# Value products of an even and an odd head alternate between the two column halves, with four buffers for turned probabilities

## The chip, the cores and the metric

The kernel runs on one core of one Trainium2 chip. The metric is the time of one execution on the device in microseconds (us); lower is better. A core has a matrix engine (TensorE, "PE" in the profile; its weight loads are listed apart as "PEld"), VectorE ("DVE"), ScalarE ("ACT"), GpSimd ("POOL") and SyncE ("SP", which only issues DMAs here). Each engine runs its own instructions in their order and waits for others on semaphores.

## The reference

One layer of a decoder on 256 tokens of width 1024. What matters here is the attention in the middle of it:

```python
h = rms_norm(x, g);  columns = h @ w_in          # queries, keys, values, gates of all branches
o_c = softmax(q k_cmp / 8 + bias) @ v_cmp        # 8 heads, 15 compressed blocks (o_c, o_s, o_w: "NSA")
o_s = softmax(q k_sel / 8 + bias, causal) @ v_sel  # 8 heads; at 256 tokens all blocks are selected
o_w = softmax(q k_win / 8 + bias, causal) @ v_win  # 8 heads
o_nsa = g0 * o_c + g1 * o_s + g2 * o_w           # gates by head and token
o_m = softmax(q k / 8 + bias, causal) @ v        # 4 heads ("moba")
o_x = softmax(q mk / 8) @ mv                     # 4 heads, 256 memory tokens ("mem")
merged = sum_i sigmoid(gate_i) * (o_i @ w_i);  x = x + rms_norm(merged @ w_mix_out)
x = x + rms_norm((silu(h @ w_gate) * (h @ w_up)) @ w_down)
```

All of it is in 32-bit floats.

## The kernel before

The wide products (`w_in`, the gates, the output projections, the feed-forward part) are each done as three products in the type fp32r: every operand is split into a high and a low part, ScalarE making the high part of a weight (`hi`, L485), VectorE the low part (`lo`, L767), and TensorE adds high by high, low by high and high by low (L1143 to L1145). The unit of this work is `sub`: 12 matmuls of 512 columns.

The attention lies in the middle of the program. Its 24 softmax products are 24 jobs, one for each head and branch (`job_plan`): 4 moba, 4 mem, then for each of the 8 NSA heads a "sel" job and a "win" job. They are run by the same loop `for n in range(JOBS + 2)` on each engine, 26 steps long, and TensorE does in step n, in this order:

- `scores(n)`: the logits of job n, four fp32r matmuls into `sbank` (L1277, L1278);
- one `sub` of a gate product, 12 matmuls into `acc`, which fills the time in which the others work on the softmax;
- `turn(n - 1)`: three or four transposes of the finished probabilities of job n - 1 from `sx` into the PSUM bank `ptb` (L1328);
- `values(n - 2)`: the products of values and turned probabilities of job n - 2.

Meanwhile VectorE adds the bias and takes the maximum (L997, L1005, L1007), ScalarE takes the exponential (L655), VectorE makes the factor (L1016, L1017, L1020), GpSimd scales the probabilities (L440), and after the transposes ScalarE copies `ptb` to SBUF as `pts`, in two buffers (`evac_pt`, L635). In step 4 four more transposes turn the compressed probabilities of all heads (L1366), after a wait for the copy of job 2.

A value product is in full fp32. The values of a head, 128 tokens by 64 dimensions, are the stationary operand; the turned probabilities, 128 tokens by 256 queries, move through. Its result takes 64 of the 128 partitions of `ob`: the lower half for an even head, the upper for an odd one. So it uses 64 of the array's 128 columns ("128*64" in the profile). A moba or win job has a product of 256 columns (L1354) and one of 128 (L1356), a mem job two of 256, a sel job three: one of 256 for the compressed branch (L1343), 256 and 128. The win job of a head adds to what its sel job left. When both halves of `ob` are complete (`ends_pair`), ScalarE and VectorE split the bank into `oh` and `ol` (L640, L1037), and the next pair's first product waits for that.

The lines that the text speaks of:

Of the kernel before, what the change touches and what calls it, by code (L numbers as in the profile page):

```python
# [25 lines left out]
F32 = mybir.dt.float32  # L26
F32R = mybir.dt.float32r
ALU = mybir.AluOpType
ACT = mybir.ActivationFunctionType
AX = mybir.AxisListType.X  # L30

P = 128
SEQ = 256
TILES = SEQ // P
D = 1024
KD = D // P
HD = 64
SCALE = HD ** -0.5
NSA_H, GROUPS, HPG = 8, 2, 4
# [13 lines left out]
C_QM, C_KM, C_VM, C_QX, C_GATES = 1304, 1560, 1816, 2072, 2328  # L53
ATT_W = C_GATES

SLICE = 512
# [11 lines left out]
JOBS = 24  # L68
# [3 lines left out]
Q_NSA, Q_MOBA, Q_MEM, Q_HEADS = 0, 8, 12, 16  # L72
# [11 lines left out]
def job_plan():  # L84

    jobs = []
    for m in range(MOBA_H):
        jobs.append(("moba", m, Q_MOBA + m, K_MOBA + m, NSA_H + m))
    for m in range(MEM_H):
        jobs.append(("mem", m, Q_MEM + m, K_MEM + m, None))  # L90
    for h in range(NSA_H):
        for kind, first in (("sel", K_SEL), ("win", K_WIN)):
            jobs.append((kind, h, Q_NSA + h, first + h // HPG, h))
    return jobs


def pair_of(job):

    return job // 2 if job < 8 else 4 + (job - 8) // 4


def ends_pair(job):

    return job % 2 == 1 if job < 8 else (job - 8) % 4 == 3
# [5 lines left out]
def t_count(job):  # L110

    return job + 1 if job < CMP_SLOT - 1 else job + 2
# [7 lines left out]
def build_layer(nc, a, out, g_scratch):  # L120
    jobs = job_plan()
# [12 lines left out]
    with ExitStack() as ctx:  # L134
        def sb(name, shape, dt=F32, stack=ctx):
            return stack.enter_context(nc.sbuf_tensor(name, shape, dt))
# [37 lines left out]
        with ExitStack() as s:  # L174

            pat = sb("pat", [P, TILES, 4 * SLICE], F32, s)
            pct = sb("pct", [P, GROUPS, SEQ], F32, s)
            kvm = sb("kvm", [P, TILES, 2 * 256], F32, s)
            with ExitStack() as early:
                x0 = sb("x0", [P, TILES, D], F32, early)  # L180
            qst = sb("qst", [P, Q_HEADS, SEQ], F32R, s)
            khh = sb("khh", [P, K_HEADS, SEQ], F32R, s)
            klo = sb("klo", [P, K_HEADS, SEQ], F32R, s)
            tb = sb("tb", [P, BIAS_H, 256], F32, s)
            tbc = sb("tbc", [P, TILES, NSA_H, 16], F32, s)
            with ExitStack() as early:
                rel = sb("rel", [BUCKETS, BIAS_H], F32, early)
                onehot = sb("onehot", [BUCKETS, SEQ], F32, early)
                grow = sb("grow", [BIAS_H, G_W], F32, early)
            with ExitStack() as early:  # L190
                kvc = sb("kvc", [P, 2, SEQ], F32, early)
                hx = sb("hx", [P, 3, 4 * NCMP], F32, early)
                hidk = sb("hidk", [P, GROUPS * NCMP], F32, early)
                hidv = sb("hidv", [P, GROUPS, HPG, 32], F32, early)
                gcmp = sb("gcmp", [P, 2, PAIRS, GROUPS * NCMP], F32, early)
            sx = sb("sx", [P, 2, 512], F32, s)
            pts = sb("pts", [P, 2, 512], F32, s)
            post = sb("post", [P, 2, CMP_LEN], F32, s)
            c_km = C_KM - SLICE
            pcz = pat[:, :, c_km:c_km + GROUPS * HPG * 32].rearrange("p t (g i c) -> p t g i c", g=GROUPS, i=HPG)  # L200
            w2k = sb("w2k", [CMP_HID, 2, HD], F32, s)
            w2v = sb("w2v", [CMP_HID, HD], F32, s)
            ckeys = sb("ckeys", [P, GROUPS, 2, 16], F32R, s)
            vcz = pat[:, :, 0:HPG * HD].rearrange("p g (i d) -> p g i d", i=HPG)
            xc = sb("xc", [P, TILES, NSA_H, 16], F32, s)
            cst = sb("cst", [P, 4, TILES * NSA_H], F32, s)
            gsig = sb("gsig", [P, TILES, 3 * NSA_H], F32, s)
            jst = sb("jst", [P, 5, JOBS, TILES], F32, s)
# [12 lines left out]
        ptb = psum("ptb", [P, 512])  # L221
        ob = psum("ob", [P, 512])
# [28 lines left out]
        qk_pe, qk_hi, qk_ev = sem("qk_pe"), sem("qk_hi"), [sem("qk_ev0"), sem("qk_ev1")]  # L251
# [6 lines left out]
        t_done, te_done, pv_done = sem("t_done"), sem("te_done"), sem("pv_done")  # L258
        oh_done, ol_done = sem("oh_done"), sem("ol_done")
# [35 lines left out]
        def half_rows(side):  # L295
            return slice(HD * side, HD * side + HD)
# [99 lines left out]
        def _(pool):  # L396
# [44 lines left out]
                                                  ALU.mult, ALU.mult)  # L441
                ins.then_inc(p_done, 1)

            pool.wait_ge(pv_done, JOBS)
            nc.gpsimd.dma_start(xs[:], xf).then_inc(xsd, 16)
            nc.gpsimd.dma_start(gpost[:], bass.AP(a["post_mix_g"].tensor, 0, [[0, P], [1, D]])).then_inc(gpostd, 16)
            for n in range(2):
# [23 lines left out]
        def _(act):  # L471
# [157 lines left out]

            def evac_pt(n):  # L630
                act.wait_ge(t_done, t_count(n))
                if n >= 2:
                    act.wait_ge(pv_done, n - 1)
                w = 512 if jobs[n][0] == "mem" else 384
                nc.scalar.activation(pts[:, n % 2, 0:w], ptb[:, 0:w], ACT.Copy).then_inc(te_done, 1)  # L635

            def evac_o(n):
                if ends_pair(n):
                    act.wait_ge(pv_done, n + 1)
                    nc.scalar.activation(oh[:, pair_of(n), :], ob[:, 0:256], ACT.Copy).then_inc(oh_done, 1)  # L640

            for n in range(JOBS + 2):
# [117 lines left out]
        def _(dve):  # L760
# [59 lines left out]
                                               ALU.mult, ALU.subtract).then_inc(meml_done, 1)  # L820

            nc.vector.memset(eps[:], EPS).then_inc(eps_set, 1)

            def reciprocals(i, slot):
                nc.vector.reciprocal(rstd[:, slot, :], small[:, 2 * i:2 * i + 2]).then_inc(rstd_done, 1)
# [313 lines left out]
        def _(pe):  # L1139
# [188 lines left out]
                    ins = nc.tensor.transpose(ptb[:, dst:dst + P], sx[:, n % 2, src:src + P], ident)  # L1328
                ins.then_inc(t_done, 1)

            def values(n):

                kind, h = jobs[n][0:2]
                starts = kind != "win"
                ends = kind != "sel"
                if n == 0:
                    pe.wait_ge(qk_ev[1], 4)
                elif ends_pair(n - 1):
                    pe.wait_ge(ol_done, pair_of(n))
                dst = ob[HD * (h % 2):HD * (h % 2) + HD]  # L1340
                if kind == "sel":
                    g = h // HPG
                    nc.tensor.matmul(dst[:, 0:256], vcz[:, g, h % HPG, :], pct[:, g, :], start=True, stop=False)  # L1343
                    starts = False
                if kind == "moba":
                    c = pat_col(C_VM + HD * h)
                    v = [pat[:, t, c:c + HD] for t in range(2)]
                elif kind == "mem":
                    v = [kvm[:, t, 256 + HD * h:256 + HD * h + HD] for t in range(2)]
                else:  # L1350
                    c = pat_col((C_VS if kind == "sel" else C_VW) + HD * (h // HPG))
                    v = [pat[:, t, c:c + HD] for t in range(2)]
                pe.wait_ge(te_done, t_count(n))
                nc.tensor.matmul(dst[:, 0:256], v[0], pts[:, n % 2, 0:256], start=starts, stop=False)  # L1354
                c0 = 0 if kind == "mem" else P
                nc.tensor.matmul(dst[:, c0:256], v[1], pts[:, n % 2, 256:512 - c0], start=False, stop=ends).then_inc(pv_done, 1)  # L1356

            for n in range(JOBS + 2):
                if n < JOBS:
# [19 lines left out]
                    qk_batch(QK_LAST, 6, [col(C_QX), col(C_QX + P)])  # L1379
                if 1 <= n <= JOBS:  # L1380
                    turn(n - 1)
                if n >= 2:
                    values(n - 2)

            def merged_banks(first, count):
# [110 lines left out]
```

## Time and profile before

| | |
|---|---|
| time, median of 3 runs | 448.36 us (448.05 to 448.48) |
| time of the profiled execution | 449.88 us |
| its span | 448.1 us |
| granted TensorE clock, mean | 0.995 |
| TensorE matmul busy | 430.5 us, 96% |
| VectorE, ScalarE, GpSimd busy | 271.7, 240.2, 57.4 us |
| the attention loop | about 92 to 209 us |

A time in a row of the timeline is the start of the first and the duration from there to the end of the last of the instructions merged in it. Matmuls are pipelined, so their durations overlap: what a matmul costs TensorE is the distance from its start to the next one's. In brackets stands how long the engine was idle before, and what released it. In rows of the trace a fp32 value product appears as two matmuls, each with its weight load (so "x2"); a transpose and a fp32r matmul appear as one.

### The profile page before, as it was taken

How to read it: one execution, taken by the hardware profiler on the slowest of the kernel's cores; microseconds unless marked ns; L12 is line 12 of the kernel's file. 1: busy time of each engine (PE TensorE's matmuls, PEld its weight loads, DVE VectorE, ACT ScalarE, POOL GpSimd, SP SyncE). 2: the span in 40 equal slices, each digit the busy share in tenths (PEclk: the TensorE clock that was granted, in tenths of full speed). 3: DMA queues.
4: the chain of work that ended last, by engine and by line, in shares of the span. 5: the costliest groups of instructions: out<-in, count | busy, mean ns of one | idle time of the engine just before them, and what ended most of it. 6: DMA issues, size and time to landing. Idle time of an engine off the chain costs nothing.

```text
span 448.1 us, 5855 instructions
## 1 busy us (share of the span) xinstructions
PE 430.5 (96%) x2044; PEld 346.3 (77%) x2044; DVE 271.7 (61%) x463; ACT 240.2 (54%) x410; POOL 57.4 (13%) x88
## 2 busy tenths in 40 slices
PE   5999979999999999999999989999999999999995
PEld 3788869977777777777778678888888888888883
DVE  4764984886556648553975956555555555545534
ACT  5655854577566564564364667444445444634321
POOL 5110720011211111111700410000000000000000
PEclk9999989999999999999999999999999999999999
DMA  8999952344522243424755347655555555555202
GB/s 303 392 327 375 364 194 95 100 135 140 189 94 96 94 113 113 151 96 148 273 166 182 123 153 236 221 186 179 175 176 175 177 179 177 181 185 193 81 1 94
DMA packets 51840, 78.80 MB, mean 176 GB/s; under 512 B 2044, under 2 KB 28424, under 8 KB 51816
## 3 DMA queue, kind: packets, MB, share of 16 engines
q1 hardware_dynamic: 50200, 73.79, 49.9%
q0 software_dynamic: 1328, 4.43, 3.0%
q8 instruction: 14, 0.23, 0.2%
q10 hardware_dynamic: 288, 0.28, 0.2%
q14 instruction: 10, 0.08, 0.1%
HBM read 77.42 MB, written 1.07 MB: 175 GB/s over the span
## 4 chain that ended last, share of the span: by engine, by line
PE 87%; DVE 5%; issue 2%; DMA 2%; ACT 1%; POOL 0%; SPq 0%; POOLq 0%; DVEq 0%; ACTq 0%
PE acc L1145 24%; PE acc L1144 24%; PE acc L1143 24%; PE ob L1354 3%; PE sbank L1277 2%; DMA raw<-in_w_in 2%; PE ptb L1328 2%; DVE wl L767 2%; PE ob L1261 2%; PE ob L1356 1%; PE sbank L1278 1%; PE ptb L1434 1%; PE ob L1343 1%; ACT wh L485 1%; PE sbank L1247 1%
## 5 line engine op out<-in xcount | busy, mean ns | idle before, releaser
L767 DVE TENSOR_TENSOR wl<-raw,wh 128x1024 fp32r<-128x1024 f32 (+1 forms) x129 | 158.3, 1234 | 92.3 <-ACT wh L485 92.1
L485 ACT ACTIVATE wh<-raw 128x1024 fp32r<-128x1024 f32 (+1 forms) x129 | 133.9, 1045 | 95.1 <-PE acc L1145 87.8
L1143 PE MATMUL acc<-wh,xh 128*128 128x512 f32 (+1 forms) x380 | 149.0, 392 | 0.6 <-DVE wl L767 0.4
L1145 PE MATMUL acc<-wh,xl 128*128 128x512 f32 (+1 forms) x380 | 149.0, 392 | 0.0
L1144 PE MATMUL acc<-wl,xh 128*128 128x512 f32 (+1 forms) x380 | 148.6, 391 | 0.0
L1143 PEld LDWEIGHTS acc<-wh,xh 128*128 128x128 f32 x380 | 72.4, 191 | 16.4 <-issue 2.2
L1145 PEld LDWEIGHTS acc<-wh,xl 128*128 128x128 f32 x380 | 71.4, 188 | 14.8
L1144 PEld LDWEIGHTS acc<-wl,xh 128*128 128x128 f32 x380 | 71.5, 188 | 13.8
L440 POOL TENSOR_SCALAR sx<-sx,jst 128x256 f32<-128x256 f32 (+1 forms) x48 | 20.2, 433 | 113.6 <-DVE jst L1017 64.1
L1143 PE MATMUL acc<-wh,ah 128*128 128x512 f32 x88 | 34.3, 390 | 0.0
L1145 PE MATMUL acc<-wh,al 128*128 128x512 f32 x88 | 34.3, 389 | 0.0
L1144 PE MATMUL acc<-wl,ah 128*128 128x512 f32 x88 | 34.2, 389 | 0.0
L655 ACT ACTIVATE sx<-sx,jst 128x128 f32<-128x128 f32 (+1 forms) x40 | 17.9, 449 | 21.4 <-DVE jst L1007 21.4
L997 DVE TENSOR_TENSOR sx<-sbank,tb 128x128 f32<-128x128 f32 (+1 forms) x40 | 12.4, 351 | 20.4 <-PE sbank L1278 20.4
L635 ACT ACTIVATE pts<-ptb 128x384 f32<-128x384 f32 (+1 forms) x24 | 12.1, 506 | 17.6 <-PE ptb L1328 17.6
L1144 PEld LDWEIGHTS acc<-wl,ah 128*128 128x128 f32 x88 | 16.5, 188 | 3.4
L1145 PEld LDWEIGHTS acc<-wh,al 128*128 128x128 f32 x88 | 16.5, 188 | 3.4
L1143 PEld LDWEIGHTS acc<-wh,ah 128*128 128x128 f32 x88 | 16.5, 188 | 3.4
L737 ACT ACTIVATE silu<-acc,rstd 128x256 f32<-128x256 f32 x22 | 10.3, 475 | 12.4 <-PE acc L1145 12.4
L1117 DVE SCALAR_TENSOR_TENSOR act_tok<-acc,rstd,silu 128x256 f32<-128x256 f32 x22 | 10.5, 481 | 7.4 <-ACT silu L737 7.4
L1277 PE MATMUL sbank<-khh,qst 128*128 128x256 f32 (+1 forms) x48 | 14.6, 329 | 0.0
L1278 PE MATMUL sbank<-klo,qst 128*128 128x256 f32 (+1 forms) x48 | 13.2, 278 | 0.0
(190 smaller groups left out, 455.8 us busy)
## 6 DMA issues: line engine op xcount, KB each, us to landing
raw<-in_w_in SPq DMA_DIRECT2D x19, 1024.0 KB
raw<-in_w_ffn_gate SPq DMA_DIRECT2D x22, 512.0 KB
raw<-in_w_ffn_up SPq DMA_DIRECT2D x22, 512.0 KB
raw<-in_w_ffn_down SPq DMA_DIRECT2D x22, 512.0 KB
raw<-in_w_mix_out SPq DMA_DIRECT2D x4, 1024.0 KB
raw<-in_w_mem_kv SPq DMA_DIRECT2D x2, 1024.0 KB
raw<-in_w_nsa_o SPq DMA_DIRECT2D x2, 1024.0 KB
tb<-g_scratch SPq DMA_DIRECT2D x1, 1536.0 KB, 17.1
```

Source lines behind the costliest of these rows:

```text
L440: ins = nc.gpsimd.tensor_scalar(sx[:, n % 2, lo:hi], sx[:, n % 2, lo:hi], jst[:, 4, n, t:t + 1], 1.0, ALU.mult, ALU.mult)
L485: nc.scalar.activation(wh[:, k, :, 0:w], raw[:, slot, 2 * half:2 * half + 2, 0:w], ACT.Copy).then_inc(hi_done, 1)
L635: nc.scalar.activation(pts[:, n % 2, 0:w], ptb[:, 0:w], ACT.Copy).then_inc(te_done, 1)
L655: ins = nc.scalar.activation(sx[:, n % 2, lo:hic], src[:, n % 2, lo:hic], ACT.Exp, bias=jst[:, 1, n, t:t + 1], scale=SCALE, accum_out=jst[ ...
L767: nc.vector.tensor_tensor(wl[:, k, :, 0:w], raw[:, slot, 2 * half:2 * half + 2, 0:w], wh[:, k, :, 0:w].bitcast(F32), ALU.subtract).then_in ...
L997: nc.vector.tensor_tensor(sx[:, n % 2, c0:c1], sbank[:, n % 2, c0:c1], tb[:, bh, c1 - c0 - 1::-1], ALU.add).then_inc(dve_c, 1)
L1143: nc.tensor.matmul(bank[:, 0:w], h[:, k, c], wh[:, slot, s, 0:w], start=first, stop=False)
L1144: nc.tensor.matmul(bank[:, 0:w], h[:, k, c], wl[:, slot, s, 0:w], start=False, stop=False)
L1145: return nc.tensor.matmul(bank[:, 0:w], l[:, k, c], wh[:, slot, s, 0:w], start=False, stop=last)
L1277: nc.tensor.matmul(dst, qst[:, q, cols], high, start=True, stop=False)
L1278: return nc.tensor.matmul(dst, qst[:, q, cols], low, start=False, stop=True)
L1354: nc.tensor.matmul(dst[:, 0:256], v[0], pts[:, n % 2, 0:256], start=starts, stop=False)
```

## The change

The jobs of heads h and h + 1 are put side by side: sel h, sel h + 1, win h, win h + 1. The value products are no longer done one job in each step, but for two jobs in every second step (n odd, from step 3 to step 25). The products of the two jobs alternate: first of the even head into the lower half of `ob`, first of the odd head into the upper half, then the second of each, and so on. For this, four buffers hold turned probabilities: the two of `pts`, now 2 x 256 columns each, and two regions of `pat` whose queries have been used by then. `evac_pt` copies all 512 columns of `ptb` always (before: 384 for all but mem jobs), so `ptb` is set to zero once at the start. `pv_done` counts pairs, and `evac_pt` waits on it from job 4 on. The first value product of each pair waits for the turned probabilities of both jobs.

```diff
--- before.py
+++ after.py
@@ -88,9 +88,10 @@
         jobs.append(("moba", m, Q_MOBA + m, K_MOBA + m, NSA_H + m))
     for m in range(MEM_H):
         jobs.append(("mem", m, Q_MEM + m, K_MEM + m, None))
-    for h in range(NSA_H):
+    for h in range(0, NSA_H, 2):
         for kind, first in (("sel", K_SEL), ("win", K_WIN)):
-            jobs.append((kind, h, Q_NSA + h, first + h // HPG, h))
+            for i in (h, h + 1):
+                jobs.append((kind, i, Q_NSA + i, first + i // HPG, i))
     return jobs
 
 
@@ -194,13 +195,15 @@
                 hidv = sb("hidv", [P, GROUPS, HPG, 32], F32, early)
                 gcmp = sb("gcmp", [P, 2, PAIRS, GROUPS * NCMP], F32, early)
             sx = sb("sx", [P, 2, 512], F32, s)
-            pts = sb("pts", [P, 2, 512], F32, s)
+            pts = sb("pts", [P, 2, TILES, 256], F32, s)
             post = sb("post", [P, 2, CMP_LEN], F32, s)
             c_km = C_KM - SLICE
             pcz = pat[:, :, c_km:c_km + GROUPS * HPG * 32].rearrange("p t (g i c) -> p t g i c", g=GROUPS, i=HPG)
             w2k = sb("w2k", [CMP_HID, 2, HD], F32, s)
             w2v = sb("w2v", [CMP_HID, HD], F32, s)
             ckeys = sb("ckeys", [P, GROUPS, 2, 16], F32R, s)
+            c_qm, c_qx = C_QM - SLICE, 3 * SLICE + C_QX - 4 * SLICE
+            turned = [pts[:, 0], pts[:, 1], pat[:, :, c_qm:c_qm + 256], pat[:, :, c_qx:c_qx + 256]]
             vcz = pat[:, :, 0:HPG * HD].rearrange("p g (i d) -> p g i d", i=HPG)
             xc = sb("xc", [P, TILES, NSA_H, 16], F32, s)
             cst = sb("cst", [P, 4, TILES * NSA_H], F32, s)
@@ -441,7 +444,7 @@
                                                   ALU.mult, ALU.mult)
                 ins.then_inc(p_done, 1)
 
-            pool.wait_ge(pv_done, JOBS)
+            pool.wait_ge(pv_done, JOBS // 2)
             nc.gpsimd.dma_start(xs[:], xf).then_inc(xsd, 16)
             nc.gpsimd.dma_start(gpost[:], bass.AP(a["post_mix_g"].tensor, 0, [[0, P], [1, D]])).then_inc(gpostd, 16)
             for n in range(2):
@@ -629,14 +632,13 @@
 
             def evac_pt(n):
                 act.wait_ge(t_done, t_count(n))
-                if n >= 2:
-                    act.wait_ge(pv_done, n - 1)
-                w = 512 if jobs[n][0] == "mem" else 384
-                nc.scalar.activation(pts[:, n % 2, 0:w], ptb[:, 0:w], ACT.Copy).then_inc(te_done, 1)
+                if n >= 4:
+                    act.wait_ge(pv_done, n // 2 - 1)
+                nc.scalar.activation(turned[n % 4], ptb[:].rearrange("p (t q) -> p t q", t=2), ACT.Copy).then_inc(te_done, 1)
 
             def evac_o(n):
                 if ends_pair(n):
-                    act.wait_ge(pv_done, n + 1)
+                    act.wait_ge(pv_done, n // 2 + 1)
                     nc.scalar.activation(oh[:, pair_of(n), :], ob[:, 0:256], ACT.Copy).then_inc(oh_done, 1)
 
             for n in range(JOBS + 2):
@@ -820,6 +822,7 @@
                                                ALU.mult, ALU.subtract).then_inc(meml_done, 1)
 
             nc.vector.memset(eps[:], EPS).then_inc(eps_set, 1)
+            nc.vector.memset(ptb[:], 0.0)
 
             def reciprocals(i, slot):
                 nc.vector.reciprocal(rstd[:, slot, :], small[:, 2 * i:2 * i + 2]).then_inc(rstd_done, 1)
@@ -1328,20 +1331,9 @@
                     ins = nc.tensor.transpose(ptb[:, dst:dst + P], sx[:, n % 2, src:src + P], ident)
                 ins.then_inc(t_done, 1)
 
-            def values(n):
+            def value_operands(n):
 
                 kind, h = jobs[n][0:2]
-                starts = kind != "win"
-                ends = kind != "sel"
-                if n == 0:
-                    pe.wait_ge(qk_ev[1], 4)
-                elif ends_pair(n - 1):
-                    pe.wait_ge(ol_done, pair_of(n))
-                dst = ob[HD * (h % 2):HD * (h % 2) + HD]
-                if kind == "sel":
-                    g = h // HPG
-                    nc.tensor.matmul(dst[:, 0:256], vcz[:, g, h % HPG, :], pct[:, g, :], start=True, stop=False)
-                    starts = False
                 if kind == "moba":
                     c = pat_col(C_VM + HD * h)
                     v = [pat[:, t, c:c + HD] for t in range(2)]
@@ -1350,10 +1342,27 @@
                 else:
                     c = pat_col((C_VS if kind == "sel" else C_VW) + HD * (h // HPG))
                     v = [pat[:, t, c:c + HD] for t in range(2)]
+                c0 = 0 if kind == "mem" else P
+                return [(v[0], turned[n % 4][:, 0], 0), (v[1], turned[n % 4][:, 1, 0:256 - c0], c0)]
+
+            def values(n):
+
+                kind = jobs[n][0]
+                if n == 1:
+                    pe.wait_ge(qk_ev[1], 4)
+                elif ends_pair(n - 2):
+                    pe.wait_ge(ol_done, pair_of(n))
                 pe.wait_ge(te_done, t_count(n))
-                nc.tensor.matmul(dst[:, 0:256], v[0], pts[:, n % 2, 0:256], start=starts, stop=False)
-                c0 = 0 if kind == "mem" else P
-                nc.tensor.matmul(dst[:, c0:256], v[1], pts[:, n % 2, 256:512 - c0], start=False, stop=ends).then_inc(pv_done, 1)
+                work = [value_operands(n - 1), value_operands(n)]
+                if kind == "sel":
+                    for w, (_k, h, *_r) in zip(work, jobs[n - 1:n + 1]):
+                        w.insert(0, (vcz[:, h // HPG, h % HPG, :], pct[:, h // HPG, :], 0))
+                for i in range(len(work[0])):
+                    for side in range(2):
+                        v, p, c0 = work[side][i]
+                        ins = nc.tensor.matmul(ob[half_rows(side), c0:256], v, p, start=(i == 0 and kind != "win"),
+                                               stop=(i == len(work[0]) - 1 and kind != "sel"))
+                ins.then_inc(pv_done, 1)
 
             for n in range(JOBS + 2):
                 if n < JOBS:
@@ -1379,7 +1388,7 @@
                     qk_batch(QK_LAST, 6, [col(C_QX), col(C_QX + P)])
                 if 1 <= n <= JOBS:
                     turn(n - 1)
-                if n >= 2:
+                if n >= 3 and n % 2:
                     values(n - 2)
 
             def merged_banks(first, count):
```

TensorE's instructions around a sel job, before, with the semaphores that they wait for (`te_done`: turned probabilities copied; `p_done`: probabilities scaled; `ol_done`: `ob` free; `e_done`: exponentials taken):

```order
L1328 MATMUL ptb<-const,sx 128x128 [waits te_done,p_done]
L1328 MATMUL ptb<-const,sx 128x128 x2
L1343 MATMUL ob<-pct,pat 64x256 [waits ol_done]
L1354 MATMUL ob<-pts,pat 64x256 [waits te_done]
L1356 MATMUL ob<-pts,pat 64x128
L1277 MATMUL sbank<-khh,qst 128x128 [waits e_done]
```

The same place in the changed kernel, the end of the step in which a pair of sel jobs is multiplied:

```order
L1331 MATMUL ptb<-const,sx 128x128 [waits te_done,p_done]
L1331 MATMUL ptb<-const,sx 128x128 x2
L1363 MATMUL ob<-pct,pat 64x256 [waits te_done,ol_done]
L1363 MATMUL ob<-pct,pat 64x256
L1363 MATMUL ob<-pts,pat 64x256 x2
L1363 MATMUL ob<-pts,pat 64x128 x2
L1280 MATMUL sbank<-khh,qst 128x128 [waits e_done]
```

The step before it now goes from the transposes straight to the next scores. In the row of `x2` the two products belong to the two heads, one in each half. Near the start of the loop, TensorE's end of step 3 and start of step 4 read so in the changed kernel:

```order
L1331 MATMUL ptb<-const,sx 128x128 [waits te_done,p_done]
L1331 MATMUL ptb<-const,sx 128x128 x2
L1363 MATMUL ob<-pts,pat 64x256 [waits te_done,qk_ev1]
L1363 MATMUL ob<-pts,pat 64x256
L1363 MATMUL ob<-pts,pat 64x128 x2
L1280 MATMUL sbank<-khh,qst 128x256 [waits e_done]
L1281 MATMUL sbank<-klo,qst 128x256
L1280 MATMUL sbank<-khh,qst 128x256
L1281 MATMUL sbank<-klo,qst 128x256
L1375 MATMUL ptb<-const,pat 128x128 [waits te_done,cmp_dve]
```

The last row is the transposes of the compressed probabilities (L1366 before); they stand where they stood, but step 2 ahead of them has lost its value products to step 3.

## Rows read from the trace of the kernel before

**Rows 1.** The page: busy time of the engines, the costliest matmul group.
```profile
PE 430.5 (96%) x2044; PEld 346.3 (77%) x2044; DVE 271.7 (61%) x463; ACT 240.2 (54%) x410; POOL 57.4 (13%) x88
...
L1143 PE MATMUL acc<-wh,xh 128*128 128x512 f32 (+1 forms) x380 | 149.0, 392 | 0.6 <-DVE wl L767 0.4
```

**Rows 2.** Busy time of the engines in the attention loop: us, busy (instructions), clock, DMA.
```profile
92.00:208.00 116.00, 116.00 (x581) 87.95 (x580) 71.01 (x190) 69.85 (x166) 20.20 (x48) 1.00 0.37 119
```

**Rows 3.** Timeline of TensorE: transposes and next scores with no value products between.
```profile
95.17 0.49 PE L1328 MATMUL ptb<-const,sx 128*128 128x128 f32 x3
95.41 0.31 PE L1277 MATMUL sbank<-khh,qst 128*128 128x128 f32 x1
```

**Rows 4.** The same with the value products of a win job.
```profile
180.22 0.49 PE L1328 MATMUL ptb<-const,sx 128*128 128x128 f32 x3
180.64 0.65 PE L1354 MATMUL ob<-pts,pat 128*64 128x256 f32 x2
181.12 0.38 PE L1356 MATMUL ob<-pts,pat 128*64 128x128 f32 x2
181.43 0.33 PE L1277 MATMUL sbank<-khh,qst 128*128 128x128 f32 x1
```

**Rows 5.** The same with those of a sel job.
```profile
184.80 0.49 PE L1328 MATMUL ptb<-const,sx 128*128 128x128 f32 x3
...
185.70 0.59 PE L1354 MATMUL ob<-pts,pat 128*64 128x256 f32 x2
186.13 0.38 PE L1356 MATMUL ob<-pts,pat 128*64 128x128 f32 x2
186.44 0.33 PE L1277 MATMUL sbank<-khh,qst 128*128 128x128 f32 x1
```

**Rows 6.** The same with those of a mem job, which has four transposes.
```profile
127.45 0.60 PE L1328 MATMUL ptb<-const,sx 128*128 128x128 f32 x4
...
128.98 0.33 PE L1277 MATMUL sbank<-khh,qst 128*128 128x128 f32 x1
```

**Rows 7.** Instructions on `ob`: count, duration ns min/median/max, first and last start.
```profile
L1354 PE MATMUL ob<-pts,pat x40: 379/379/431, 99.2 to 208.3; 128*64 128x256 f32 x40
...
L1343 PE MATMUL ob<-pct,pat x16: 379/404/431, 137.5 to 204.1; 128*64 128x256 f32 x16
...
L1354 PE MATMUL ob<-pts,kvm x8: 379/404/430, 118.2 to 133.0; 128*64 128x256 f32 x8
```

**Rows 8.** Timeline of the weight loads within the win job's value products.
```profile
180.64 0.19 PEld L1354 LDWEIGHTS ob<-pts,pat 128*64 128x64 f32 x2 [0.17 <-issue]
180.91 0.35 PEld L1356 LDWEIGHTS ob<-pts,pat 128*64 128x64 f32 x2
```

**Rows 9.** Timeline around steps 2 to 4, all engines.
```profile
98.77 0.55 PE L1328 MATMUL ptb<-const,sx 128*128 128x128 f32 x3
...
100.48 0.82 POOL L440 TENSOR_SCALAR sx<-sx,jst 128x128 f32<-128x128 f32 x2 [1.77 <-DVE jst L1020]
...
103.39 0.49 PE L1328 MATMUL ptb<-const,sx 128*128 128x128 f32 x3
...
104.15 0.47 ACT L635 ACTIVATE pts<-ptb 128x384 f32<-128x384 f32 x1
...
105.17 0.60 PE L1366 MATMUL ptb<-const,pat 128*128 128x128 f32 x4
```

**Rows 10.** Timeline: the softmax of the job whose scores start at 181.43, and its transposes.
```profile
182.19 0.62 DVE L997 TENSOR_TENSOR sx<-sbank,tb 128x128 f32<-128x128 f32 x2 [1.79 <-PE sbank L1278]
...
185.06 0.82 POOL L440 TENSOR_SCALAR sx<-sx,jst 128x128 f32<-128x128 f32 x2 [3.73 <-DVE jst L1017]
...
189.79 0.49 PE L1328 MATMUL ptb<-const,sx 128*128 128x128 f32 x3
```

**Rows 11.** VectorE's first work after the start of the program.
```profile
4.89 0.48 DVE L814 SCALAR_TENSOR_TENSOR xl<-gx,xh 128x256 fp32r<-128x256 f32 x1 [4.01 <-ACT xh L525]
```

## Prediction

> **What bounds the kernel now.** I read the page first. TensorE is busy for 96% of the span, no other engine for more than 61%, and the costliest matmul group was idle for 0.6 us in all [rows 1]. Then the busy times of the attention loop, the only stretch that the change touches: from 92 to 208 us TensorE is busy in every one of 116.00 us, at a granted clock of 1.00, which is its 2.4 GHz level; VectorE has 71.01 us of work there, ScalarE 69.85, the DMA engines are used to 37% [rows 2]. So in this loop a microsecond less on TensorE is a microsecond less of time, until another engine's latency shows. Last the timeline at the end of a step, since a busy matrix engine says nothing of what each product costs it: there I take distances between starts.
>
> **What a block of value products costs.** From the first transpose to the next scores TensorE needs 95.41 - 95.17 = 0.24 us when no value product stands between [rows 3]. With a win job it is 181.43 - 180.22 = 1.21 us [rows 4], so the block costs 0.97. With a sel job it is 186.44 - 184.80 = 1.64 [rows 5], block 1.40. With a mem job 128.98 - 127.45 = 1.53 [rows 6]; one transpose more is about 0.11 of that (three of them and the switch take 0.42 to the first value product [rows 4]), block 1.18. A moba job has a win job's products: 0.97.
>
> Inside a block a 256-column product costs 186.13 - 185.70 = 0.43 [rows 5], and one of 128 columns half of it, 0.21. Then a win block streams 0.64, a sel block 1.07, a mem block 0.85, and what remains is 0.33 in each of the three. That is the price of going into the 128*64 shape and out again: 0.18 ahead of the first product (180.64 - 180.22 against 0.24), the rest behind the first weight load and after the last product. The whole: 12 x 0.97 + 8 x 1.40 + 4 x 1.18 = 27.6 us, of which 24 x 0.33 = 7.9 is switching and 19.6 streaming (rounded).
>
> **Part 1, half as many blocks.** The jobs are multiplied in pairs, 12 blocks for 24. If the 0.33 is paid once for a block, 12 x 0.33 = 4.0 us go. This needs nothing but that alternating between the halves is no switch of its own.
>
> **Part 2, two halves of the array.** The trace of before has no place where products for different halves stand next to each other, so the gain is bounded: nothing at the one end (they run one after the other, as two products of one half do at 0.43 apart [rows 5]), half the streaming time at the other, 19.6 / 2 = 9.8 us. A loss is possible too, and is a rival below. Between the ends I take this. A fp32 product is two matmuls in the trace, each with its weight load (40 for 20 jobs) [rows 7], at 0.213 each for 256 columns, 0.107 for 128. Matmuls start in program order, and the order is A1 A2 B1 B2 with A and B the two heads. A2 has to wait for A1, since both use the lower half. B1 can start with A2, and A's next product with B2. In slots of one 256-column matmul:
> - win or moba pair: A1 | A2 B1 | B2 and the first short one of A | then, at 0.107 each, the second short one of A, and B's two, the first of which waits for B2: 0.213 x 3 + 0.107 x 2 = 0.85, against 2 x 0.64;
> - mem pair: four products, 5 slots, 1.07, against 1.71;
> - sel pair: 5 slots and 0.21 for the last short ones, 1.28, against 2.13.
>
> With 0.33 each, a win or moba pair costs 1.18 instead of 1.94, a mem pair 1.40 instead of 2.36, a sel pair 1.61 instead of 2.80. The gain is 6 x 0.76 + 2 x 0.96 + 4 x 1.19 = 11.3 us (4.0 of it is part 1). I take this value because pipelining in order is what every row of TensorE shows, and the weight load of a following product already runs beside the matmul in flight (below).
>
> The Trainium skill speaks on both sides. "TensorEngine Tiling (Array Packing)", Key Properties, says that tiles of one mode execute loads and matmuls in parallel and that only a change of mode drains the engine; by it the gain is between 11.3 and 13.8. "TensorE: Matmul & The Clock Gate", Part 3, says that a weight load overlaps matmuls in flight only if its row group differs, and here both halves use all rows; by that every change of half would expose a load, and the gain would be no more than that of part 1. The trace of before disagrees with the latter in one half at least: the weight load of L1356 starts at 180.91 [rows 8], while the product ahead of it runs until its successor's start at 181.12 [rows 4]. No row shows it for two halves.
>
> **Part 3, the copies of turned probabilities.** 20 of the 24 copies take 512 columns for 384: at most 0.47 x 128/384 = 0.16 us each, 3.1 us more on ScalarE. Its 69.85 us of 116 [rows 2] hide this. Four buffers relax the wait on `pv_done`. Clearing `ptb` is one VectorE instruction ahead of everything, where that engine is idle for 4.01 us [rows 11]: nothing.
>
> **Part 4, new waits.** In the even steps TensorE now comes to the next transposes earlier, in the odd ones later. In a steady step the softmax has room: scores start at 181.43, GpSimd ends at 185.06 + 0.82 = 185.88, and the transposes of that job start at 189.79 [rows 10], 3.9 us later. Two steps get shorter by some 0.8 to 1.2 us together, so 2.7 us remain. One place is tight, the start of the loop, where the others lag. Step 2 has no value products any more, so the transposes of step 3 start at 103.39 - 0.97 = 102.42 (their probabilities are ready at 101.30) [rows 9]. Then 0.24, the first pair's 1.18, and the scores of step 4, which take 105.17 - 103.39 - 1.21 = 0.57: TensorE is at the transposes of the compressed probabilities at 104.41. These wait for the copy of job 2, which stands on ScalarE behind an exponential that hangs on VectorE and ends at 104.62 [rows 9], with 0.16 for its length at 104.78. TensorE waits 0.4 us. Behind it on TensorE is a `sub` and everything else, so all of it counts.
>
> What follows the loop moves forward as a whole. GpSimd's load of `xs` waits for the last value product before and after alike; no DMA is added, and at 37% the queue has room for a loop that is 9% shorter.
>
> **The sum.** 449.88 (the profiled execution; its span of 448.1 and 1.8 around it) - 11.3 + 0.4 = 439.0. The profiled execution was 1.5 above the median of the runs, 448.36, and against that the forecast is 437.5 us.
>
> **The rivals.**
> - *Both halves fully side by side*, without the stagger: A1 with B1. For it: both halves are free at the start of a block. Against it: A2 stands ahead of B1 and would have to be passed. Every pair's block costs one job's: 27.6 / 2 = 13.8, less a wait of 0.6 in step 4 (TensorE is there 0.2 earlier): 435.2 us.
> - *The halves do not overlap*, only the switching is halved. For it: nothing in the trace shows overlap in fp32. 448.36 - 4.0 = 444.4; TensorE then comes to step 4's transposes at 104.8, and the wait is nil.
> - *Overlap, but part of it given back*: the shorter even steps run into VectorE, above all in steps 17 and 18, where it also merges gate products, or each pair starts slower than I think. Against it are the 2.7 us of room. I price it at 2 to 4 us of the 11: 439.5 to 441.5.
> - *Slower: a change of half costs as much as a change of shape.* The place is between any two products of a pair: 3 changes in a moba, mem or win pair (8 pairs), 5 in a sel pair (4 pairs), 44 in all. With one way of a switch at 0.33 / 2 = 0.17 that is 7.5 us, less the 4.0 saved: 451.9. It decides from 0.09 us for a change on. For it: the way in and out of the 128*64 shape costs something, so the array does drain at some changes. Against it: the shape stays the same here.
>
> **How the numbers follow.** Chances: staggered overlap 50%, full overlap 7%, overlap partly given back 8%, none 27%, slower 8%. The predicted time is 437.5. The likeliest case's own range is 436.0 to 439.5. The range for 8 in 10 runs from the full overlap, 435.0, to the case without overlap, 445.0; only the slower case and tails lie outside. This kernel's measurement tells 0.2% (0.9 us) from no change. All cases but one are faster by more; for mishaps that eat the 4.0 I take 3% for no change: faster 0.89, same 0.03, slower 0.08.
>
> **What would show it.** In the profile after: the distance from transposes to next scores in odd steps, 0.24 + 1.18 (win), 0.24 + 1.61 (sel), and 0.24 in even ones; within a pair, starts of value matmuls closer than 0.213 with two in flight, at the same granted clock of 1.00. Distances of 0.43 for each product would show no overlap, gaps ahead of each weight load on `ob` the slower case. The transposes of the compressed probabilities should wait 0.4 us for ScalarE's copy. If TensorE had idle time in the loop beyond this, part 4 would be wrong; if the part of the program from the last value product on were longer than before, the assumption that it moves as a whole would be.

## The result and the profile after

| | before | changed |
|---|---|---|
| median of 4 runs | 448.38 us (448.05 to 448.48) | 435.86 us (435.16 to 436.66) |
| ratio | | 0.9714, 95% interval 0.9693 to 0.9735 |
| profiled execution; its span | 449.88; 448.1 | 435.16; 433.4 |

The forecast was 437.5 us in a range of 435.0 to 445.0. The time lies in the range, 1.6 us below the forecast, close to the rival of full overlap (435.2).

The changed kernel's runs lie in two pairs (435.16, 435.20; 436.51, 436.66), and 435.86 is the middle between them. The two profiles differ in the same way, so their spans are 14.7 us apart, more than the change is worth. The stretch that makes the difference lies ahead of the attention. In the profile of before, the row of 60 to 70 us:

```profile
60.00:70.00 10.00, 9.36 (x50) 8.12 (x51) 5.74 (x10) 7.58 (x13) 0.53 (x1) 0.83 0.60 206
```

In that of the changed kernel:

```profile
60.00:70.00 10.00, 9.32 (x59) 8.32 (x60) 5.74 (x9) 7.54 (x13) 0.53 (x1) 1.00 0.59 205
```

The number after the five engines is the granted clock: a mean of 0.83 in the one, so a part of the stretch at 1.2 GHz, and 1.00, 2.4 GHz, in the other. The same work is there at the same place. Of the eleven profiles of this case, the five with 0.83 in that row have the first scores of the loop at 91.67 to 92.01 us, the six with 1.00 at 90.03 to 90.29, whichever kernel it is. In both profiles here TensorE had stood idle just before 60.6 us, for 2.5 us before and 2.4 after, so the idle time alone doesn't decide it; why the clock fell in one and not in the other is open. The first scores start at 91.85 before and at 90.29 after, 1.56 us earlier, and none of that is the change.

The rest of the 14.7 us is in the loop. From the first scores to the last block of value products it takes 208.08 - 91.85 = 116.23 us before and 193.34 - 90.29 = 103.05 after, 13.18 less. From there to the end it is 240.0 us in one and 240.1 in the other, so what follows moved forward as a whole. The page's busy row, which answers to the first of [rows 1]:

```profile
PE 415.7 (96%) x2044; PEld 338.6 (78%) x2044; DVE 272.0 (63%) x464; ACT 241.7 (56%) x410; POOL 57.4 (13%) x88
```

TensorE is as busy as before by share; the same 2044 matmuls take 14.8 us less, some 1.6 of it from the clock between 60 and 70 us. In the loop, against [rows 2], by the same columns:

```profile
92.00:193.00 101.00, 100.48 (x567) 79.92 (x566) 69.97 (x187) 70.04 (x162) 20.23 (x48) 1.00 0.42 135
```

The other engines do the same work in 101 us that took them 116; TensorE is idle for 0.52 us, where it had not been at all.

The timeline of TensorE in the changed kernel shows where the time went. The rows are, in order, a mem pair, a sel pair, a step without value products and a win pair, to be read as [rows 3 to 6]:

```profile
118.51 0.60 PE L1331 MATMUL ptb<-const,sx 128*128 128x128 f32 x4
119.03 1.08 PE L1363 MATMUL ob<-pts,kvm 128*64 128x256 f32 x8
120.05 0.33 PE L1280 MATMUL sbank<-khh,qst 128*128 128x128 f32 x1
...
135.44 0.49 PE L1331 MATMUL ptb<-const,sx 128*128 128x128 f32 x3
135.86 0.65 PE L1363 MATMUL ob<-pct,pat 128*64 128x256 f32 x4
136.34 0.82 PE L1363 MATMUL ob<-pts,pat 128*64 128x256 f32 x8
137.09 0.33 PE L1280 MATMUL sbank<-khh,qst 128*128 128x128 f32 x1
...
140.44 0.49 PE L1331 MATMUL ptb<-const,sx 128*128 128x128 f32 x3
140.69 0.31 PE L1280 MATMUL sbank<-khh,qst 128*128 128x128 f32 x1
...
144.03 0.49 PE L1331 MATMUL ptb<-const,sx 128*128 128x128 f32 x3
144.45 0.87 PE L1363 MATMUL ob<-pat 128*64 128x256 f32 x8
145.25 0.33 PE L1280 MATMUL sbank<-khh,qst 128*128 128x128 f32 x1
```

From transposes to next scores a win pair takes 1.22 us, where one win job took 1.21 [rows 4]; a sel pair 1.65, where one job took 1.64 [rows 5]; a mem pair 1.54, where one took 1.53 [rows 6]; a step without, 0.25. Two jobs cost what one had cost. How the two halves run is seen in the instructions of that line in flight at the start of the win pair (kind, name, count; durations in ns; first and last start):

```profile
L1363 PEld LDWEIGHTS ob<-pat x4: 133/134/136, 144.5 to 144.5; 128*64 128x64 f32 x4
L1363 PE MATMUL ob<-pat x2: 430/430/430, 144.5 to 144.5; 128*64 128x256 f32 x2
```

Two matmuls of 256 columns have started within the resolution of the row, each at the 430 ns that a single one takes too, and the weight loads of all four matmuls of the two products have started as well. The row doesn't say which half a matmul uses. But in the kernel before, where the four matmuls of a win job are all for one half, a window of 0.3 us from 180.6 holds only one:

```profile
L1354 PE MATMUL ob<-pts,pat x1: 430/430/430, 180.6 to 180.6; 128*64 128x256 f32 x1
```

So the two that start together in the changed kernel are one of each half. The one new wait on TensorE in the loop is the expected one:

```profile
PE ptb L1375 <- ACT pat L637: 0.5, 1, 0.5
```

It costs a little more than it shows. From the last score ahead of these transposes to the first of them TensorE takes 103.31 - 102.51 = 0.80 us, where it took 105.17 - 105.06 = 0.11 in the kernel before: 0.7 us.

### The profile page after: what moved, and what is told of

It is laid out like the page before. It is cut to its first block, busy times and chain, and to the rows that moved or that the text cites. A ratio compares the mean times of both kernels' runs of the same rounds, so it can differ in the third digit from the quotient of the medians.

```text
span 433.4 us, 5858 instructions
## 1 busy us (share of the span) xinstructions
PE 415.7 (96%) x2044; PEld 338.6 (78%) x2044; DVE 272.0 (63%) x464; ACT 241.7 (56%) x410; POOL 57.4 (13%) x88
## 2 busy tenths in 40 slices
DMA packets 51840, 78.80 MB, mean 182 GB/s; under 512 B 2044, under 2 KB 28424, under 8 KB 51816
## 3 DMA queue, kind: packets, MB, share of 16 engines
HBM read 77.42 MB, written 1.07 MB: 181 GB/s over the span
## 4 chain that ended last, share of the span: by engine, by line
PE 86%; DVE 7%; issue 3%; ACT 2%; DMA 1%; POOL 1%; POOLq 0%; DVEq 0%; ACTq 0%
PE acc L1148 25%; PE acc L1147 25%; PE acc L1146 25%; PE ob L1363 3%; DVE wl L769 2%; PE ptb L1331 2%; PE ob L1264 2%; PE sbank L1280 1%; PE ptb L1443 1%; PE sbank L1281 1%; ACT wh L488 1%; DMA gx<-in_gx 1%; PE sbank L1250 1%; DVE gates L982 1%; POOL yb L462 1%
## 5 line engine op out<-in xcount | busy, mean ns | idle before, releaser
L1147 PEld LDWEIGHTS acc<-wl,xh 128*128 128x128 f32 x380 | 71.6, 188 | 13.8
L1281 PE MATMUL sbank<-klo,qst 128*128 128x256 f32 (+1 forms) x48 | 13.1, 278 | 0.0
L685 ACT ACTIVATE tmp<-acc 128x512 f32<-128x512 f32 x8 | 4.8, 598 | 14.6 <-PE acc L1148 14.6
```

The costliest lines, as they stand in the source:

```text
L1147: nc.tensor.matmul(bank[:, 0:w], h[:, k, c], wl[:, slot, s, 0:w], start=False, stop=False)
L1281: return nc.tensor.matmul(dst, qst[:, q, cols], low, start=False, stop=True)
```

## Experiments

The medians below carry the 1.5 us of the stretch from 60 to 70 us in some runs and not in others. The profiles are free of it from the first scores of the loop to the end of the span, and each has a granted clock of 1.00 in the whole loop:

| kernel | first scores to end, us | against changed |
|---|---|---|
| before | 356.2 | +13.1 |
| changed | 343.1 | |
| heads_in_turn | 345.0 | +1.9 |
| one_half | 352.3 | +9.2 |
| job_by_job | 356.2 | +13.1 |
| full_width | 348.8 | +5.7 |
| two_by_two | 343.1 | 0.0 |
| changed_again | 343.1 | 0.0 |
| slot6 | 342.4 | -0.7 |
| quads | 341.7 | -1.4 |
| quads_slot6 | 341.0 | -2.1 |

**Three kernels that undo one thing each, and one that takes the shape away.** They ran on one chip. The first keeps all and lets the heads of a pair follow one another:

```diff
-                for i in range(len(work[0])):
-                    for side in range(2):
+                for side in range(2):
+                    for i in range(len(work[0])):
```

> The changed kernel, but in each pair all products of the even head stand first, then all of the odd head: same products, same blocks, same halves. Theory 1 (the two halves run side by side, and what they do is bounded only by each half's own work): it depends on whether the second head's first product may start before the first head's last has been issued. If TensorE issues matmuls strictly in program order, only the last matmul of one head meets the first of the other: a win or moba pair costs 1.28 - 0.11 + 0.33 = 1.5 us for 0.97, a sel pair 2.36 for 1.40, a mem pair 1.82 for 1.18, in all about 6 x 0.53 + 4 x 0.96 + 2 x 0.64 = 8.3 us more than the changed kernel: about 444. If each half has a queue of its own that is filled ahead, it costs nothing: 435.9. Rival (the gain is from fewer blocks and from more room for the other engines, and not from overlap): no change against the changed kernel, 435.9, with pairs at 1.0 us in a trace that shows no two matmuls of different halves together.

Measured: 437.4 us median (437.12 to 438.79), ratio to before 0.9737 [0.9714, 0.9760]; span 435.3 against 433.4. Neither 444 nor 435.9. The blocks tell why. A sel pair and a win pair:

```profile
135.44 0.49 PE L1331 MATMUL ptb<-const,sx 128*128 128x128 f32 x3
135.86 0.65 PE L1363 MATMUL ob<-pct,pat 128*64 128x256 f32 x2
136.34 0.38 PE L1363 MATMUL ob<-pts,pat 128*64 128x256 f32 x1
136.35 0.43 PE L1363 MATMUL ob<-pct,pat 128*64 128x256 f32 x1
136.56 0.38 PE L1363 MATMUL ob<-pts,pat 128*64 128x256 f32 x1
...
136.77 0.87 PE L1363 MATMUL ob<-pts,pat 128*64 128x128 f32 x6
137.57 0.33 PE L1280 MATMUL sbank<-khh,qst 128*128 128x128 f32 x1
...
144.51 0.49 PE L1331 MATMUL ptb<-const,sx 128*128 128x128 f32 x3
144.94 0.88 PE L1363 MATMUL ob<-pat 128*64 128x256 f32 x8
145.75 0.33 PE L1280 MATMUL sbank<-khh,qst 128*128 128x128 f32 x1
```

The win pair takes 1.24 us, full overlap, although the whole first head stands ahead of the second in the program. Two of its matmuls start together here too:

```profile
L1363 PE MATMUL ob<-pat x2: 430/430/430, 144.9 to 145.0; 128*64 128x256 f32 x2
```

A mem pair, with two products of 256 columns for each head, takes 1.55 for 1.54. In the sel pair, with three products for each head, the odd head's first product (the second row of `pct`) starts at 136.35, together with the even head's second (136.34) and ahead of the even head's third; the pair takes 2.13 for 1.65. Four times 0.48 is the 1.9 us. So TensorE does start a product ahead of earlier ones that wait for their own half. With two products of one half ahead it does so at once; with three, the other half starts only when the first of the three is through. What stands ahead of the prediction, that each engine runs its instructions in their order, doesn't hold for TensorE where two halves are in use. A strict program order is refuted. So is the rival that nothing is gained from overlap: its time of 435.9 is not met, and the operand names show products of both heads under way at once.

The second writes both heads' products to the lower half, each overwriting the last. So the odd heads' results and the sums are left out:

```diff
-                        ins = nc.tensor.matmul(ob[half_rows(side), c0:256], v, p, start=(i == 0 and kind != "win"),
-                                               stop=(i == len(work[0]) - 1 and kind != "sel"))
+                        ins = nc.tensor.matmul(ob[half_rows(0), c0:256], v, p, start=True,
+                                               stop=True)
```

> The changed kernel, but the products of both heads go to the lower half of the bank and each overwrites what was there (the odd heads' results and the sums are left out of what is computed); number, order, shapes and waits of all instructions are as in the changed kernel. Theory 1 (overlap of the halves): the overlap is gone, and 9.8 us come back: about 445.7, that is 435.9 + 9.8, and every pair's block costs twice its streaming time, 1.28 + 0.33 for a win pair. Rival (fewer blocks and room for the others): no change, 435.9.

Measured: 445.92 us median (444.16 to 445.98), ratio 0.9917 [0.9900, 0.9934]; span 442.4. Its win pair:

```profile
147.26 0.49 PE L1331 MATMUL ptb<-const,sx 128*128 128x128 f32 x3
147.68 1.51 PE L1363 MATMUL ob<-pat 128*64 128x256 f32 x8
149.13 0.33 PE L1280 MATMUL sbank<-khh,qst 128*128 128x128 f32 x1
```

1.87 us for 1.22, so a block of 1.62, near 2 x 0.64 + 0.33. From the first scores to the end it is 9.2 us longer than the changed kernel: all overlap gone, 9.8 us, less the 0.7 of the wait in step 4, which goes too when TensorE comes later. That the overlap is between the halves is shown by this: the instructions, their order and their waits are the same, and only the half and the flags that begin and end a sum differ. That the median lies so near the 445.7 expected is in part chance, since three of the four runs have a mean clock of 0.992 to 0.995 and the fourth, at 1.000, took 444.16.

The third keeps the order of jobs, the four buffers, the wide copies and the cleared bank, and goes back to one job in each step:

```diff
-                work = [value_operands(n - 1), value_operands(n)]
+                work = [value_operands(n)]
...
-                if n >= 3 and n % 2:
+                if n >= 2:
                     values(n - 2)
```

> The changed kernel with its order of jobs, its four buffers, its wider copies and the cleared bank, but the products of one job in every step as before, each head in its own half. Theory 1: everything but the pairing is worth nothing, so the time is that of the kernel before, 448.4 (447.8 to 449.0). Rival (part of the gain is from buffers and looser waits): below that, 444 or less.

Measured: 449.16 us median of 10 runs (448.21 to 450.30) beside 449.93 for the kernel before (448.33 to 450.11, 13 runs), ratio 0.9990 [0.9974, 1.0007]. From the first scores to the last block it takes 207.94 - 91.71 = 116.23 us, to the hundredth what the kernel before takes. All of the change but the pairing is worth nothing that can be measured.

The fourth is the kernel before with value products of 128 columns for 64, which write the whole bank. The values of the neighbour head are multiplied too, so it doesn't compute the layer's attention:

```diff
-                dst = ob[HD * (h % 2):HD * (h % 2) + HD]
+                dst = ob
...
-                    v = [kvm[:, t, 256 + HD * h:256 + HD * h + HD] for t in range(2)]
+                    v = [kvm[:, t, 256 + P * (h // 2):256 + P * (h // 2) + P] for t in range(2)]
```

> The kernel before, but each value product takes 128 columns of values (its head's and its neighbour's) and writes all 128 partitions, so its results are those of the wrong sums; streamed columns, number and order of instructions are the same, only the 128*64 shape and the way into and out of it are gone. Theory 1 (0.33 us of each block is the change of shape): 24 x 0.33 = 7.9 us less, about 440.5; the distance from transposes to next scores with a win job falls from 1.21 to 0.88. Rival (the 0.33 is the price of any change from transposes to fp32 products): no change, 448.4.

Measured: 441.70 us median (440.71 to 443.84), ratio 0.9838 [0.9802, 0.9873]; span 439.0 at a clock of 0.999. The block of a win job:

```profile
137.74 0.49 PE L1328 MATMUL ptb<-const,sx 128*128 128x128 f32 x3
138.06 0.60 PE L1354 MATMUL ob<-pts,pat 128*128 128x256 f32 x2
138.64 0.31 PE L1277 MATMUL sbank<-khh,qst 128*128 128x128 f32 x1
```

0.90 us for 1.21 [rows 4]: 0.31 of the 0.33 is the change of shape. From the first scores to the end it is 7.4 us shorter than before, and 24 x 0.31 is 7.4.

**How far TensorE looks ahead.** One more order of the same products, A the even head and B the odd one:

```diff
-                for i in range(len(work[0])):
-                    for side in range(2):
+                order = [(0, 0), (0, 1), (1, 0), (1, 1), (0, 2), (1, 2)][:6 if kind == "sel" else 4]
+                for side, i in order:
```

> The changed kernel, with the six products of a sel pair in the order A A B B A B (A the even head, B the odd one), and the four of the other pairs in the order A A B B. Theory 1, as it stands after the run with the heads in turn (TensorE looks ahead past two products of one half, four matmuls, but not past three): full overlap everywhere, a sel pair at 1.65 us from transposes to next scores, as when the heads alternate. Rival (any second product of one half in a row costs something): between 1.65 and the 2.13 us that A A A B B B costs, near 1.9.

Measured: one run, 436.62 us, and 343.1 us from the first scores to the end, as in the changed kernel. Its sel pair:

```profile
136.84 0.49 PE L1331 MATMUL ptb<-const,sx 128*128 128x128 f32 x3
137.26 0.66 PE L1363 MATMUL ob<-pct,pat 128*64 128x256 f32 x4
137.74 0.83 PE L1363 MATMUL ob<-pts,pat 128*64 128x256 f32 x8
138.50 0.33 PE L1280 MATMUL sbank<-khh,qst 128*128 128x128 f32 x1
```

1.66 us, full overlap. Two products of one half in a row cost nothing, three do. What the limit counts is not shown: products, their matmuls (two each) and weight loads go together in all of these orders. Nor do they separate a limit in number from one in time, between the 0.85 us that two products of a mem job stream and the 1.07 of three of a sel job.

**A version beyond the change.** Two things were left: the wait of 0.5 us in step 4, and 12 changes of shape. Three further kernels ran on one chip with the changed kernel itself.

> The changed kernel itself, timed beside the three below on one chip. All theories: 0.971 of the time of before, as measured first.

Measured: 435.11 us median (434.93 to 436.65), ratio to before 0.9694 [0.9668, 0.9719].

```diff
-CMP_SLOT = 4
+CMP_SLOT = 6
```

> The changed kernel with the compressed probabilities turned in step 6 instead of step 4 (CMP_SLOT = 6, which also moves VectorE's work for them from step 2 to step 4). Theory 1: the wait of TensorE ahead of these transposes, 0.52 us in the profile of the changed kernel, is real time, and goes: 0.5 us less than the changed kernel, some 0.999 of it. Rival (the wait only moves, to the transposes of another job or to the new place): no change, with another wait of about 0.5 in the trace.

Measured: 436.14 us median (435.97 to 436.38), ratio to before 0.9707 [0.9683, 0.9731]. By the medians that is 1.0 us slower, but all five runs have a mean clock of 0.994 to 0.996, and the profiled one has 0.83 between 60 and 70 us. The changed kernel has one run of five like that here, 436.65. From the first scores to the end slot6 is 0.7 us shorter, for 0.5 expected: the whole 0.7 that the wait costs by distance. The wait ahead of the compressed transposes is gone, and TensorE has no other in its place:

```profile
PE ob L1250 <- DVE xc L967: 0.5, 1, 0.5
```

This is the one that the loop starts with, in the changed kernel too. The wait and what it costs in the loop are shown; five runs of one sort don't show the gain in the time of the whole.

The next kernel joins the blocks of the sel pair and the win pair of the same two heads:

```diff
-                if n >= 3 and n % 2:
+                if n in (3, 5, 7, 9):
                     values(n - 2)
+                elif n >= 13 and n % 4 == 1:
+                    values(n - 4)
+                    values(n - 2)
```

> The changed kernel, but for the NSA heads the sel pair and the win pair of the same two heads are multiplied in one block, in every fourth step: 8 blocks for 12, with the same products. Theory 1: 4 x 0.33 = 1.3 us less than the changed kernel, since only the change of shape is saved. Rival (a block of ten products holds up a copy of turned probabilities: the next job's must wait for the first pair, as all four buffers are full, and ScalarE behind it is late for the softmax): no gain, or a wait of TensorE for probabilities or for the copy in the step after each block.

Measured: 434.50 us median (433.63 to 436.48), ratio to before 0.9679 [0.9652, 0.9707]. The medians differ by 0.6 us, but the loop is 1.4 us shorter, for 1.3 expected. Its mean clock is no guide here: the profiled run, 433.77, has a mean of 0.996 and yet 1.00 between 60 and 70 us; it lost clock at the very end, 0.90 after 415 us.

The last takes both edits.

> Both of the last two. Theory 1: the gains add, 1.8 us less than the changed kernel. Rival: no more than the better of the two alone.

Measured: 433.22 us median (433.00 to 434.87), ratio to before 0.9647 [0.9624, 0.9671]. That is 1.9 us less than the changed kernel on that chip, and 2.1 from the first scores to the end, where the two gains alone are 0.7 and 1.4: the gains add. This is the best version. A double block in it, at the end of step 13:

```profile
143.44 0.49 PE L1331 MATMUL ptb<-const,sx 128*128 128x128 f32 x3
143.86 0.65 PE L1363 MATMUL ob<-pct,pat 128*64 128x256 f32 x4
144.34 0.82 PE L1363 MATMUL ob<-pts,pat 128*64 128x256 f32 x8
144.99 0.82 PE L1363 MATMUL ob<-pat 128*64 128x256 f32 x8
145.74 0.33 PE L1280 MATMUL sbank<-khh,qst 128*128 128x128 f32 x1
```

2.30 us for sel and win pair, which took 1.65 + 1.22 - 0.25 = 2.62 apart. The rival of the run with both pairs in one block spoke of ScalarE. Its waits (who waited for whom, total us, times, longest) have this row:

```profile
ACT pts L637 <- PE ob L1363: 5.9, 3, 2.1
```

The copy does wait for the value products, up to 2.1 us, because all four buffers are full. TensorE is not kept by it, with no wait in the loop but the one at its start: the rival had the wait right and its consequence wrong.

## Why the prediction came out as it did

- *TensorE bounds the loop, and its time is the kernel's.* Right: 13.18 us went from the loop, and no more than 0.1 came back behind it.
- *Price of a block.* Right. 0.97, 1.40 and 1.18 were read from distances of starts, and 0.33 of each as switching; with 128 columns 0.31 goes, and with one half the pair costs twice the streaming and once the switching (1.62 for 1.61).
- *Part 1, half as many blocks, 4.0 us.* Right, with no price on changing the half. The run with one half has no overlap and half the blocks, and is 356.2 - 352.3 = 3.9 us shorter than the kernel before.
- *Part 2, overlap.* This is the term that was mis-sized: 7.3 us were put for it (11.3 with part 1), and it is 9.8: the run with one half is 9.2 us longer than the changed kernel, and has not the 0.7 of the wait. The step that failed is "Matmuls start in program order, and the order is A1 A2 B1 B2". B's first matmul does not wait for A's second; it starts with A's first, as the profile shows, and it does so even with a second product of A ahead of it. Taking the pipelining of one shape as a proof of order was the error: in the trace of before nothing ever stood behind a matmul that waited for a half it did not need. The sum with the full overlap was in the prediction already, as a rival with 7%: 27.6 / 2 = 13.8, less 0.6. Measured, the wait costs 0.7, and 13.8 less 0.7 is 13.1 for the 13.18 of the loop. (The prediction's own products, 6 x 0.76 + 2 x 0.96 + 4 x 1.19, add up to 11.2 and not 11.3.)
- The Trainium skill, in "TensorEngine Tiling (Array Packing)", Key Properties, has it that tiles of one mode load and multiply in parallel; this case agrees (1.22 us for two jobs for 1.21 for one). Its "TensorE: Matmul & The Clock Gate", Part 3, states that matmuls start and end in the order of the program, and that loads overlap matmuls in flight only where the row groups differ. The runs differ from both, and the measurement decides. Loads of both halves, which share all rows, start within 0.1 us of the two matmuls in flight. With the heads in turn, a matmul of the second half started at 136.35, and the second matmul of the product ahead of it at 136.56.
- *Part 3, copies and clearing at no cost.* Right: 0.9990 [0.9974, 1.0007] with all of that and without the pairs.
- *Part 4, a wait of 0.4 us in step 4.* Right in place and cause. TensorE stood idle for 0.52 and lost 0.7 by the distance of starts, more than forecast, in part because with full overlap it comes there earlier. No other wait came, though VectorE and ScalarE now do their 70 us of work in 101.
- *The slower rival*, a price on each change of half, did not happen: 44 changes of half cost nothing that the distances show (1.22 against 1.21).
- *The medians.* I took the sum from the profiled time and went down by 1.5 us to the median. The changed kernel's median fell between its two pairs of runs, 0.7 us above the 435.2 that the full overlap gives, which made the forecast look nearer than its reasons were. Profile against profile the forecast was 439.0, and 435.16 came: 3.8 lower, 2.5 of it the overlap and 1.6 the clock from 60 to 70 us, less 0.3 for the longer wait. That the forecast is only 1.6 us off is luck in part: the case that I held likeliest did not happen, and the case that did had 7%.

## What to carry to other kernels

Where products use 64 of the array's columns, bring two that use different halves next to each other: a pair costs what one did, also in fp32 of two matmuls a product. Alternate them, or keep no more than two of one half in a row, and gather them in few blocks, for each way into the narrow shape and out again cost 0.3 us here. To size such a thing beforehand, take the distance from the last instruction ahead of the block to the first behind it, with and without the block, and split it into streaming and switching by comparing blocks of different length.

## What the runs showed of the hardware that I had not expected

- Two matmuls for different column halves of one PSUM bank run fully side by side, at 430 ns each for the first, with four weight loads started, at no loss against one alone (1.22 us for 1.21).
- TensorE starts a product of one half ahead of earlier products of the other half: past two of them at once (1.24 us for a win pair in order A A B B), but past three only when the first is through (2.13 for 1.65 us in order A A A B B B).
- Into the 128*64 shape and back costs 0.31 us at 2.4 GHz, between transposes and fp32r products that use all 128 columns (1.21 us for a win job, 0.90 in full width).
- A part of the stretch from 60 to 70 us runs at 1.2 GHz in five of eleven profiles and not in the others, with TensorE idle for 2.4 to 2.5 us ahead of it in one of either sort. It moves the start of the loop by 1.4 to 2.0 us, more than the last edits here are apart, so profiles are to be compared from behind it. The mean clock of a run alone doesn't tell: one of the quickest runs had 0.996.
